# A seven-product MLP: the positive part moved to ScalarE without its norm factor, the squared factor applied at the end, and three of four down pairs crossed

## What is computed

```python
def rmsnorm(x, g, eps=EPS):
    y = x * lax.rsqrt(jnp.mean(x * x, axis=-1, keepdims=True) + eps)
    return y * g
...
def sq_relu_mlp(y, w_up, w_down):                  # w_up 1024 x 4096, w_down 4096 x 1024
    return jnp.square(jax.nn.relu(y @ w_up)) @ w_down
...
for i in range(DEPTH):                             # DEPTH = 2
    h = h + mixer_i(rmsnorm(h, norm_gains[i, 0]))
    h = h + sq_relu_mlp(rmsnorm(h, norm_gains[i, 1]), mlp_w_up[i], mlp_w_down[i])
return rmsnorm(h, final_gain)[:, N_META:]
```

## Time and profile before

| | us |
|---|---|
| median of 3 runs | 1199.21 (1197.19 to 1201.06) |
| the profiled execution, its own time | 1197.49 |
| its span in the trace | 1195.6 |
| TensorE busy in the span | 1175.9 |
| VectorE busy | 957.5 |
| ScalarE busy | 741.5 |

### The profile page before, as it was taken

How to read it: one execution, slowest core, us unless ns; L and a number is a source line. 1 busy time by engine, 2 the same in 40 slices (tenths; PEclk the granted TensorE clock), 3 DMA queues, 4 the chain that set the end, 5 groups by cost and what they waited for, 6 DMA issues and landing times. The chain is left out here.

```text
span 1195.6 us, 22842 instructions
## 1 busy us (share of the span) xinstructions
PE 1175.9 (98%) x8809; PEld 1125.9 (94%) x8809; DVE 957.5 (80%) x1423; ACT 741.5 (62%) x1305; POOL 114.5 (10%) x171
## 2 busy tenths in 40 slices
PE   9999999999999999999999999999999999999998
PEld 8999999999999999999999999987788988989988
DVE  6889898887788787786568889887878887978953
ACT  5777877645565564565357887877555555645643
POOL 3211110100110110111010000000001001001000
PEclk9999999999999999999999999999999999999999
DMA  7343342432553453583132122214335536445622
GB/s 180 93 111 86 88 112 74 155 100 72 143 143 107 107 143 107 114 230 121 54 90 70 54 70 70 88 50 132 103 106 111 142 104 151 130 124 133 196 80 71
DMA packets 152374, 131.87 MB, mean 110 GB/s; under 512 B 23208, under 2 KB 143072, under 8 KB 152288
## 3 DMA queue, kind: packets, MB, share of 16 engines
q1 hardware_dynamic: 141600, 104.93, 30.6%
q0 software_dynamic: 10560, 25.66, 9.4%
q10 hardware_dynamic: 128, 0.09, 0.0%
HBM read 111.43 MB, written 19.24 MB: 109 GB/s over the span
## 5 line engine op out<-in xcount | busy, mean ns | idle before, releaser
L2042 PE MATMUL ps<-yh,wh 128*128 128x264 f32 (+1 forms) x704 | 160.5, 302 | 0.0
L2042 PE MATMUL ps<-yh,wl 128*128 128x264 f32 (+1 forms) x704 | 155.3, 295 | 0.0
L2042 PE MATMUL ps<-yl,wh 128*128 128x264 f32 (+1 forms) x704 | 155.3, 295 | 0.0
L1654 DVE TENSOR_TENSOR lo<-lof,hi 128x1024 fp32r<-128x1024 f32 x80 | 97.0, 1223 | 51.9 <-ACT hi L762 51.9
L2325 PE MATMUL ps<-th,hi 128*128 128x264 f32 (+1 forms) x448 | 126.9, 283 | 2.7 <-DVE ps L1679 2.7
L2325 PE MATMUL ps<-tl,hi 128*128 128x264 f32 (+1 forms) x448 | 126.5, 282 | 0.0
L2325 PE MATMUL ps<-th,lo 128*128 128x264 f32 (+1 forms) x448 | 126.4, 282 | 0.0
L762 ACT ACTIVATE hi<-lof 128x1024 fp32r<-128x1024 f32 x80 | 82.2, 1054 | 65.1 <-DVE lof L1647 65.0
L762 ACT ACTIVATE hi<-raw 128x1024 fp32r<-128x1024 f32 (+1 forms) x128 | 114.0, 914 | 9.9 <-DMA raw<-in_mlp_w_up_dram 9.5
L2277 PE MATMUL ps<-ah,hi 128*128 128x264 f32 (+1 forms) x448 | 115.6, 316 | 0.0
L2277 PE MATMUL ps<-al,hi 128*128 128x264 f32 (+1 forms) x448 | 115.6, 316 | 0.0
(11 more groups left out here) (325 smaller groups left out, 3288.6 us busy)
## 6 DMA issues: line engine op xcount, KB each, us to landing
raw<-in_mlp_w_up_dram SPq DMA_DIRECT2D x32, 1024.0 KB, 6.4
raw<-in_mlp_w_down_dram SPq DMA_DIRECT2D x32, 1024.0 KB, 5.0
raw<-in_diff_w_in_dram SPq DMA_DIRECT2D x24, 512.0 KB, 3.8
raw<-in_mlstm_w_in_dram SPq DMA_DIRECT2D x16, 512.0 KB, 4.4
h_sum<-abuf POOLq DMA_DIRECT2D x24, 264.0 KB, 7.0
h_sum<-abuf POOLq DMA_DIRECT2D x24, 256.0 KB, 6.9
h_sum<-h POOLq DMA_DIRECT2D x16, 264.0 KB, 2.4
h<-h_sum POOLq DMA_DIRECT2D x2, 2112.0 KB, 12.7
```

The lines of the kernel that those rows point to most:

```text
L1654: V.tensor_tensor(lo[1 - i % 2][:, rows, :], lof[1 - i % 2][:, rows, :], hi[1 - i % 2][:, rows, :].bitcast(F32), ALU.subtract).then_inc(m_ ...
L2042: last = mm(ps[:, bank + s, 0:w_], w[:, slot, kb, :], m[:, kb, t0:t0 + w_], start=(kb == 0 and n == 0), stop=(kb == CB - 1 and n == 2))
```

## The change

- `DOWN_FROM` goes from 6 to 5: in the first three groups of each layer three of four down pairs are crossed, i % 8 = 5 being the first. The activation forms are made one pair earlier.
- The positive part of an up pair is taken by ScalarE, unscaled, right before its two squares. VectorE has no eviction in up pairs any more.
- The norm factor is applied, squared, at the end (`rb` holds the inverse mean square itself for these norms). So the sum of the first three groups is kept by itself in `h_sum`, while `h` is kept in `h_kept`. In the last group GpSimd's queue loads the eight rows of `h_sum` back one by one into two buffers, and VectorE multiplies each by `rb` and adds it to `h` (`add_sum`), two rows ahead of each of the first four evictions. Each of the eight last evictions is a multiplication by `rb` and an addition.
- VectorE makes C22 ahead of C1 in every crossed pair; in the first crossed down pair it comes between `form_lo(i+1, "S14")` and `block_lo` A22.

```diff
 PLAIN = 2
-DOWN_FROM = 6
+DOWN_FROM = 5
 PAIRS = 8 * GROUPS
...
 SENT_OUT = counted((i, m) for i in range(PAIRS) if sent_down(i) for m in range(2))
 RANK = counted(i for i in range(PAIRS) if crossed(i))
 COPIED = counted((i, e) for i in range(PAIRS) if crossed(i) for e in ("P1", "P5", "U2"))
-ADDED = counted((i, e) for i in range(PAIRS) if crossed(i) for e in (("C1", "C22") if crossed(i + 1) else ("C22", "C1")))
+ADDED = counted((i, e) for i in range(PAIRS) if crossed(i) for e in ("C22", "C1"))
 SENT = counted(i for i in range(PAIRS) if sent_down(i))
 STEP = (counted(("gain_t", "meta_t0", "gate_mm", "u_t", "m_spread")) | counted(("hm_rd", "ym_hi", "ucol_rd"))
         | counted(("gain_rd", "ym_made", "gwh_done", "gw_ready", "ym_lo")))
+LAST = counted((k, e) for n in range(CB) for k, e in
+               ([(2 * n, "mul"), (2 * n, "add"), (2 * n + 1, "mul"), (2 * n + 1, "add")] if n < 4 else []) + [(n, "row")])
+N_LAST = len(LAST)
 N_DONE, N_READY, N_TAKEN, N_OUT, N_CROSSED, N_COPIED, N_ADDED, N_SENT = (
     len(x) for x in (DONE, READY, TAKEN, SENT_OUT, RANK, COPIED, ADDED, SENT))
 SLOT = {"A11": 0, "A12": 1, "S2": 2, "S3": 3, "S1": 4, "S4": 5, "A22": 6}
...
         p5 = [place("p50", [P, HALF], F32, r0, ring_at + 2 * RING * CB * P * 4)]
         tb = [tbuf, place("tbuf1", [P, T], F32, w0, limit)]
         ab = [abuf, place("abuf1", [P, T], F32, w0, limit)]
+        last_sum = [tb[1], ab[1]]
         p5.append(place("p51", [P, HALF], F32, w0, limit))
         w0 = [a_at]
         gx, gabs, gexp, gln, glf, gone = (place(n, [64, T], F32, w0, a_end)
...
         fin = place("fin", [P, 4, D], F32, [arena], limit)
         ps = ctx.enter_context(nc.psum_tensor("ps", [P, 8, 512], F32))
-        h_sum = nc.dram_tensor("h_sum", [CB, P, T], F32).ap()
+        h_kept, h_sum = (nc.dram_tensor(n, [CB, P, T], F32).ap() for n in ("h_kept", "h_sum"))
         gate_rows = nc.dram_tensor("gate_rows", [2 * HEADS, T], F32).ap()
         def sem(name):
...
         def sent_before(layer, i):
-            return 16 * (N_SENT * layer + SENT[i] - 1)
+            return 16 * ((N_SENT + CB // 2) * layer + SENT[i] - 1)
+
+        def all_sent(layer):
+
+            return 16 * ((N_SENT + CB // 2) * layer + N_SENT)
         def freed(layer, i, m):
...
                 t0 = mlp_shape(layer)[0]
                 for k in range(CB):
                     pool.wait_ge(h_ready, 16 * layer + k + 1)
-                    pool.dma_start(h_sum[k], h[:, k, :]).then_inc(h_saved, 16)
+                    pool.dma_start(h_kept[k], h[:, k, :]).then_inc(h_saved, 16)
                 pool.wait_ge(h_saved, 16 * CB * (layer + 1))
                 for i in range(PAIRS):
                     for m in range(2):
                         if not sent_down(i):
                             continue
                         pool.wait_ge(m_out, N_OUT * layer + SENT_OUT[i, m])
-                        pool.dma_start(h_sum[2 * (i % 8) - 8 + m, :, t0:T], ab[m][:, t0:T], accum_op=ALU.add).then_inc(h_sent[m], 16)
+                        row = h_sum[2 * (i % 8) - 8 + m, :, t0:T]
+                        if i < 8:
+                            pool.dma_start(row, ab[m][:, t0:T]).then_inc(h_sent[m], 16)
+                        else:
+                            pool.dma_start(row, ab[m][:, t0:T], accum_op=ALU.add).then_inc(h_sent[m], 16)
                 pool.wait_ge(m_done, N_DONE * layer + DONE[PAIRS - 9, "A22"])
                 for m in range(2):
-                    pool.wait_ge(h_sent[m], 16 * N_SENT * (layer + 1))
-                pool.dma_start(h[:, :, :], h_sum.rearrange("k p t -> p k t")).then_inc(h_back, 16)
+                    pool.wait_ge(h_sent[m], all_sent(layer))
+                pool.dma_start(h[:, :, :], h_kept.rearrange("k p t -> p k t")).then_inc(h_back, 16)
+                pool.wait_ge(a_ready, 32 * (layer + 1))
+                for k in range(CB):
+                    wait(pool, last_step, N_LAST * layer + LAST[k - 2, "add"] if k >= 2 else 0)
+                    pool.dma_start(last_sum[k % 2][:, t0:T], h_sum[k, :, t0:T]).then_inc(h_sent[k % 2], 16)
             residuals(0)
             pool.wait_ge(m_done, DONE[PAIRS - 5, "A22"])
...
                 src = ps[:, bank:bank + 2, 0:HALF] if len(spans) == 2 else ps[:, bank, 0:X]
                 nc.scalar.activation(tokens(rb[:, :], spans), src, ACT.Ln, bias=eps_d[:, 0:1], scale=1.0 / D).then_inc(ln_done, 1)
                 act.wait_ge(ln_done, n + 1)
-                nc.scalar.activation(tokens(rb[:, :], spans), tokens(rb[:, :], spans), ACT.Exp, scale=-0.5).then_inc(rb_ready, 1)
+                nc.scalar.activation(tokens(rb[:, :], spans), tokens(rb[:, :], spans), ACT.Exp,
+                                     scale=-1.0 if n % 2 else -0.5).then_inc(rb_ready, 1)
             nc.scalar.preload_act_table_set("natural_log_exp_and_others")
...
                     k = 2 * (i % 8) + m
                     b = 8 * (4 * layer + i // 8) + k
+                    if not crossed(i):
+                        act.wait_ge(m_done, items + DONE[i, m])
+                    else:
+                        if m == 1:
+                            act.wait_ge(m_done, items + DONE[i, "A22"])
+                        act.wait_ge(c_done, adds + ADDED[i, "C22" if m else "C1"])
+                    nc.scalar.activation(pair_tokens(tb[m], layer, i), pair_out(layer, i, m), ACT.Relu).then_inc(m_evac, 1)
                     act.wait_ge(m_evac, layer * N_TAKEN + TAKEN[i, m])
                     wait(act, a_ready, b - 1)
                     if i == 0:
...
                     elif i % 8 == 0:
                         act.wait_ge(m_done, items + DONE[i - 1, "A22"])
                     if i == PAIRS - 8:
-                        act.wait_ge(h_sent[m], 16 * N_SENT * (layer + 1))
+                        act.wait_ge(h_sent[m], all_sent(layer))
                     nc.scalar.activation(square_out(layer, i, m), halves(tb[m][:, t0:T]), ACT.Square).then_inc(sqa_done, 1)
                     nc.scalar.activation(ah[:, k, t0:T], tb[m][:, t0:T], ACT.Square).then_inc(ah_done, 1)
...
                 t0, w = mlp_shape(layer)
                 mid = t0 + w
                 items, ranks, norm = layer * N_DONE, layer * N_CROSSED, 2 * layer + 1
-                copies, adds = layer * N_COPIED, layer * N_ADDED
+                copies, adds, t_in = layer * N_COPIED, layer * N_ADDED, spans[0][0]
                 def form(i, name, after):
...
                     V.tensor_tensor(blocks_r[:, :, n, 0:w], blocks_f[:, :, n, 0:w], block_form(layer, name).bitcast(F32),
                                     ALU.subtract).then_inc(b_lo, 1)
+                def add_sum(k):
+
+                    s = last_sum[k % 2]
+                    dve.wait_ge(h_sent[k % 2], all_sent(layer) + 16 * (k // 2 + 1))
+                    V.tensor_tensor(s[:, t_in:T], s[:, t_in:T], rb[:, t_in:T], ALU.mult).then_inc(last_step, 1)
+                    dve.wait_ge(last_step, N_LAST * layer + LAST[k, "mul"])
+                    V.tensor_tensor(h[:, k, t_in:T], h[:, k, t_in:T], s[:, t_in:T], ALU.add).then_inc(last_step, 1)
+
                 def evacuate(i, m):
-                    if crossed(i):
-                        if m == 1:
-                            dve.wait_ge(m_done, items + DONE[i, "A22"])
-                        dve.wait_ge(c_done, adds + ADDED[i, "C22" if m else "C1"])
-                    else:
-                        dve.wait_ge(m_done, items + DONE[i, m])
-                    src = pair_out(layer, i, m)
-                    if is_up(i):
-                        if (i, m) == (0, 0):
-                            dve.wait_ge(rb_ready, norm + 1)
-                        wait(dve, ah_done, block_of(i, m) - 1)
-                        V.scalar_tensor_tensor(pair_tokens(tb[m], layer, i), src, 0.0, pair_tokens(rb, layer, i),
-                                               ALU.max, ALU.mult).then_inc(m_evac, 1)
-                        return
                     k = 2 * (i % 8) + m - 8
-                    dve.wait_ge(h_back, 16 * (layer + 1))
-                    V.tensor_tensor(tokens(h[:, k, :], spans), src, tokens(h[:, k, :], spans), ALU.add).then_inc(m_evac, 1)
+                    if k == 0:
+                        dve.wait_ge(rb_ready, norm + 1)
+                        dve.wait_ge(h_back, 16 * (layer + 1))
+                    if k < 4:
+                        add_sum(2 * k)
+                        add_sum(2 * k + 1)
+                    dve.wait_ge(m_done, items + DONE[i, m])
+                    V.tensor_tensor(tokens(tbuf, spans), pair_out(layer, i, m), tokens(rb, spans), ALU.mult).then_inc(last_step, 1)
+                    dve.wait_ge(last_step, N_LAST * layer + LAST[k, "row"])
+                    V.tensor_tensor(h[:, k, t_in:T], tbuf[:, t_in:T], h[:, k, t_in:T], ALU.add).then_inc(m_evac, 1)
                     if i >= PAIRS - 4:
                         dve.wait_ge(m_evac, layer * N_TAKEN + TAKEN[i, m])
...
                     if i == 0:
```

(23 more changed lines are left out.)

8 lines of the change are left out of this document (6 added, 2 removed).

## The result

The changed kernel takes 1211.0 us (median of 4 runs, 1210.7 to 1215.6) and the kernel before, beside it, 1200.1 (1197.2 to 1203.4). The ratio is 1.0089, with a 95% interval of 1.0068 to 1.0110: slower by 0.9%. Predicted were 1205.0 us and a range that ended at 1210, so the direction was right and the size was not. The working had found 6.8.

The account below looks back on a forecast made before the run. TensorE, busy 98% of the span, was taken as the bound. Terms -8.1 - 3.3 - 8.7 + 13.2 + 10.1 + 3.6 = +6.8 us gave 1204.3 profiled, 1206.0 as median; predicted 1205, range 1194 to 1210.

Parts of the forecast that it names:

- The old waits at A22: First crossed down pair of each group: C22 ahead of C1 removes TensorE's six waits, 8.7 us less.
- among the up pairs: TensorE's four waits on sums among up pairs go, with order changed and VectorE's evictions gone: 3.3 us less.
- The ends: Last group of each layer: VectorE's added multiplications and additions delay TensorE, 10.1 us in layer 1, 3.6 in layer 0.
- The row loads: Reloads of 264 KB rows at each layer's end: a little over 2.4 us each, hidden up to some 3.5.
- the last group has room: Rival: the added sums fit VectorE's idle time, leaving 0.4 us of 13.7 at the ends; 1192 us, chance 0.15.
- the forms are on time at S3: Rival: VectorE's queue in iteration 12 is 2.4 us shorter, 13.2 less; 1192 us, chance 0.06.
- slow row loads: Rival: row loads at the layers' ends land in 7 us; 1212 us, chance 0.08.
- the term of the first crossed down pair: VectorE's longer queue makes TensorE wait in each group, 2.0 us in layer 0, 2.4 in layer 1: 13.2 more.
- The wait at S3: First crossed down pair: TensorE waits for VectorE's S3 residue, 1.8 us in layer 0, 2.2 in layer 1.
- 0.1 more latency at each of ten hand-overs: Upper bound at the first crossed down pair: 1.0 us more per group, 6 us more in all.
- The end of layer 0: Block 7 of attention's first projection waits 3.2 us for VectorE; GpSimd's masks add 0.4, from nothing to 0.7; together 3.6.
- ScalarE as the bound: Rival: ScalarE's positive part and squares delay each of 28 crossed up pairs by 0.3, 8 us; 1213, chance 0.04.

Follow-up runs that it names:

- part 3: Changed kernel with two of four down pairs crossed: 1203.0 us; changed kernel with the reloaded rows neither multiplied nor added: 1197.7 us.
- Part 5: Changed kernel with the next pair's A11 ahead of S3 in the first crossed down pair: 1208.7 us.
- part 6: Changed kernel, three versions: forms for S1 and A22 left out, 1199.4 us; form for A22 on GpSimd, 1218.2; layer 0's GpSimd masks moved earlier, 1210.3.
- part 7: Kernel before with C22 first everywhere and residual rows returned in eight transfers: 1188.0 us; that with the third pair crossed, 1206.0; with one transfer, 1193.1.
- part 1: Kernel before with C22 made ahead of C1 in every crossed pair, nothing else changed: 1196.8 us.
- parts 4: Changed kernel with the remainder for S3 moved ahead of the form of pair 6 and its like: 1213.0 us.
- 2: Kernel before with only the third of four down pairs crossed as well: 1214.5 us.
- the last but one of 7: Kernel before with C22 first, eight return transfers, the third pair crossed and A11 ahead of S3: 1206.0 us.

## Why the prediction was right in direction and short in size

**Right.** The old waits at A22 and among the up pairs went. The ends cost what they should, and for the reason given: additions that an in-order queue can't put into its idle time, in a step bound by VectorE and ScalarE in turn. Layer 1 measures 10.6 for 10.1. Less the 3.1 us by which pair 28 began late, the first three tail products start at 1167.0, 1174.5 and 1179.0 for 1166.9, 1174.4 and 1178.7. Only the idle times ahead of them are not as forecast, 3.7, 3.1 and none for 3.5, 4.7 and 1.6. The first two products ran in part at the lower clock and took some 4.4 us each in place of 2.84, in time that TensorE would else have spent idle. In part 3's kernel with two pairs the second of them keeps the upper clock, the third waits 1.2 us, and the end costs the same 10.5. The row loads landed in 3.0 to 4.7 us (medians 3.1 to 3.4) and were hidden. ScalarE, 66% busy, is nowhere the bound of the up pairs, and its positive part takes 0.6 us there, as its copies do, with no pause ahead of it for a change of table. The rivals "the last group has room", "the forms are on time at S3" and "slow row loads" did not come.

**The step that failed** is the term of the first crossed down pair, "2.0 x 3 + 2.4 x 3 = 13.2 us more". It measures 19.1. The wait at S3 itself was right: 1.9 and 2.4 us for 1.8 and 2.2, 12.8 in six. What follows was 0.45 a group and not 0.2: the next S2 is 0.27 late, as worked out, and the two products that restart after an idle engine another 0.1 each; with the 0.1 to 0.2 by which S3 waited longer that is 2.3 more in all. The rest, 3.6 us, is TensorE's clock, of which the working had nothing: it took each product after a wait at its usual 1.42 us. Part 5 shows the 3.6 alone. The bound that was kept for this place ("0.1 more latency at each of ten hand-overs") was wide enough for the sum, 6 us, but named another cause, and the range ended at 1210, 1 us short of the 1211 that this bound gives with 1205.

**The end of layer 0** was "3.2" plus 0.4 for the masks; it measures 5.1, and three instructions beside the masks are 1.67 longer, which with the 3.2 makes 4.9. "Nothing to 0.7" was a guess without a row. The masks, like VectorE's remainders, read and write SBUF, and what two such instructions do to each other is seen in two of part 6's runs. The wait of 3.1 at the projection's first block, which the working hadn't named, lies ahead of the 1.4 at block 7 and adds nothing to it: the last `yl` sets the end of both.

**The sum.** Measured as offsets: -0.3 before pair 0, -3.4 in the up pairs (-3.3 was taken), +1.7 in the six stretches of down pairs (-8.1 - 8.7 + 13.2 = -3.6 was taken), +5.1 and +10.6 at the ends: 13.7. Inside the 1.7 the loss of the groups rises from 9.2 (8.7 was taken; the rest is 0.1 a group at S2) to 19.1, and the other 8.2 won is the products of the third pair, for 8.1. So the forecast of 6.8 was short by 5.9 at S3, by 1.5 at the end of layer 0 and by 0.5 at that of layer 1, less small terms the other way.

That 1205 was 6.0 short of the measured 1211.0 and not 6.9 is chance. The working put the profiled execution after at 1204.3 and added 1.7, by which the one before lay under its median. The one after took 1211.0 and lay at its median, so that the 1206.0 of the working was 5.0 short; the 1205 predicted takes off another 1.0 for which it gives no reason. The measured time lies beside two rivals at 1212 and 1213, slow row loads and ScalarE as the bound, neither of which came.

**What the edits are worth,** in spans: the sums in the new order -9.4 (part 7 with eight transfers, where no accident hides it); the two ends +15.5; the third pair +9.0 (both from part 3). With the 13.7 of the whole change this leaves -1.4 for the positive part on ScalarE, which was not run alone. It fits the up pairs, which win 3.4 with it and 2.0 by order alone (part 1).

**Why the third pair loses** is settled as far as this: between pair 4 and pair 6 VectorE has more to do than TensorE's time allows, by the greater part of the 2.35 and 2.83 us; the last 1.0 is its turns with ScalarE (part 6). The wait moves with the order (parts 4 and 5), keeps its sum where VectorE's order is kept (5), shrinks with less work and grows with more (6, 2, and the last but one of 7). What stays open is why the clock falls in three groups of six after waits of 1.9 and 2.4 us: the changed kernel with its masks moved, which has the same six waits, shows it in one.

## What to carry to other kernels

When an in-order queue is late, move one instruction and look at the *sum* of the waits behind it: if it does not fall, the engine may be short of time there; then take work out, and see whether the sum falls by as much. A factor that is moved to the end is cheap only if the work that it leaves for the end fits into real gaps of the engine that does it; here 24 added instructions in layer 0 and 28 in layer 1 cost 5.1 and 10.6 us on an engine that was 81% busy, in gaps that were there but in the wrong places. After each edit look for a transfer that now starts just ahead of another: a gain of 3 us in order can be lost to a load that is issued half a microsecond too late.

## What was not expected of the hardware

- TensorE's granted clock fell to its lower level after single waits of 1.9 to 2.4 us in a stretch that was otherwise full, in three of six places that look alike, at 1.2 us each. Three waits of 0.4 to 1.3 us with the same sum did not bring it down in any of six. After waits of 3.7 and 3.1 us in the tail of layer 1 it fell too, and cost nothing, since the next product had to wait anyway.
- A GpSimd subtraction of 128 x 1024 took 3.31 us, and held VectorE's for 2.2 us.
- A weight load of 1 MB took 12.0 to 12.5 us when it was issued 0.5 to 0.7 us behind a transfer of 2.1 MB, and 6.0 to 7.0 when issued 0.2 us behind it or ahead, seven times and five times in layer 0. Beside the same 2.1 MB in eight parts, the first of them issued 0.5 us ahead of it, the load took 8.5 us, and TensorE did not wait there.
